# The last expert's last row of w_down multiplied by activations summed into tokens, and four stores of 256 KB

## What is computed

```python
def expert_block(args):
    e, toks, gw = args
    xb = h[toks]
    gu = xb @ w_gu[e] + b_gu[e]
    gate = jnp.minimum(gu[:, :D_FF], SWIGLU_LIMIT)
    up = jnp.clip(gu[:, D_FF:], -SWIGLU_LIMIT, SWIGLU_LIMIT)
    act = gate * jax.nn.sigmoid(gate * SWIGLU_ALPHA) * (up + 1.0)
    y = act @ w_down[e] + b_down[e]
    return (y * gw[:, None]).astype(h.dtype)
...
return jax.ops.segment_sum(y.reshape(n_slots, -1), slot_tok, num_segments=T)
```

## Time and profile before

| | |
|---|---|
| median of 3 runs | 989.25 us (989.24 to 989.61) |
| the profiled execution | 988.7 us |
| its span, first to last instruction | 986.9 us |
| mean granted TensorE clock | 0.987 |
| TensorE busy | 946.6 us, 96% |
| VectorE, ScalarE busy | 202.9 us, 127.7 us |
| HBM read | 416.80 MB, 423 GB/s over the span |

### The profile page before, as it was taken

How to read it: one execution, slowest core, us unless ns; L and a number is a source line. 1 busy time by engine, 2 the same in 40 slices (tenths; PEclk the granted TensorE clock), 3 DMA queues, 4 the chain that set the end, 5 groups by cost and what they waited for, 6 DMA issues and landing times.

```text
span 986.9 us, 11112 instructions
## 1 busy us (share of the span) xinstructions
PE 946.6 (96%) x4508; PEld 382.4 (39%) x4508; DVE 202.9 (21%) x610; ACT 127.7 (13%) x346; POOL 14.0 (1%) x9
## 2 busy tenths in 40 slices
PE   9999999999999899898989989889989999999997
PEld 5545433333333334333333333333333333333432
DVE  4645121212111121210112121011212112111121
ACT  2433111011110111010011101001101110011101
POOL 0031000000000000000000000000000000000000
PEclk9999999999999999999999999999999999999999
DMA  9999999999999999999999999999999999999996
GB/s 374 426 423 398 412 429 434 432 430 428 432 431 429 436 430 430 434 432 429 434 433 426 437 432 428 437 430 429 436 429 431 432 429 430 431 433 430 422 422 272
DMA packets 23869, 418.27 MB, mean 424 GB/s; under 512 B 2912, under 2 KB 3296, under 8 KB 8224
## 3 DMA queue, kind: packets, MB, share of 16 engines
q1 hardware_dynamic: 23408, 417.20, 99.2%
q10 hardware_dynamic: 432, 0.66, 0.2%
HBM read 416.80 MB, written 1.05 MB: 423 GB/s over the span
## 4 chain that ended last, share of the span: by engine, by line
PE 63%; DMA 36%; DVE 1%; issue 0%; ACT 0%; SPq 0%; DVEq 0%
DMA ring<-w_gu_dram 33%; PE ps L1237 29%; PE ps L1342 14%; PE ps L1205 4%; PE ps L1189 4%; DMA ring<-w_down_dram 3%; PE ps L1066 3%; PE ps L997 2%; PE ps L1004 1%; PE ps L1293 1%; PE ps L1301 1%; PE ps L1013 0%; PE ps L1039 0%; PE ps L1058 0%; PE ps L1046 0%
## 5 line engine op out<-in xcount | busy, mean ns | idle before, releaser
L1237 PE MATMUL ps<-ring,passing 128*64 128x512 f32 x1008 | 229.1, 604 | 14.8 <-DMA ring<-w_gu_dram 14.8
L1237 PE MATMUL ps<-ring,PR 128*64 128x512 f32 x976 | 224.5, 608 | 16.4 <-DMA ring<-w_gu_dram 16.2
L1342 PE MATMUL ps<-ring,PT 128*64 128x512 f32 x984 | 218.3, 595 | 0.5 <-DMA ring<-w_down_dram 0.5
L952 DVE TENSOR_SCALAR xw<-ps 128x256 f32<-128x256 f32 x64 | 27.2, 425 | 650.0 <-PE ps L1237 650.0
L1237 PEld LDWEIGHTS ps<-ring,passing 128*64 128x64 f32 x1008 | 76.8, 139 | 158.3 <-issue 143.8
L1237 PEld LDWEIGHTS ps<-ring,PR 128*64 128x64 f32 x976 | 74.9, 140 | 157.0 <-issue 145.4
L1342 PEld LDWEIGHTS ps<-ring,PT 128*64 128x64 f32 x984 | 68.1, 137 | 129.6 <-issue 127.5
L652 ACT ACTIVATE xw<-xw 128x256 f32<-128x256 f32 x64 | 26.6, 416 | 484.5 <-DVE xw L952 484.5
L1205 PE MATMUL ps<-PT 64*128 64x512 f32 x248 | 69.7, 640 | 0.0
L1189 PEld LDWEIGHTS ps<-qk,X 128*128 128x128 f32 x512 | 59.6, 191 | 18.8 <-issue 18.8
L1189 PE MATMUL ps<-qk,X 128*128 128x128 f32 x512 | 65.7, 281 | 0.0
(11 more groups left out here) (198 smaller groups left out, 374.6 us busy)
## 6 DMA issues: line engine op xcount, KB each, us to landing
ring<-w_gu_dram SPq DMA_DIRECT2D x48, 4096.0 KB, 28.2
ring<-w_down_dram SPq DMA_DIRECT2D x25, 4096.0 KB, 29.7
ring<-w_gu_dram SPq DMA_DIRECT2D x14, 2048.0 KB, 14.2
ring<-w_gu_dram SPq DMA_DIRECT2D x6, 3072.0 KB, 23.2
ring<-w_down_dram SPq DMA_DIRECT2D x5, 2048.0 KB, 23.1
ring<-w_gu_dram SPq DMA_DIRECT2D x9, 1024.0 KB, 9.6
ring<-w_down_dram SPq DMA_DIRECT2D x8, 1024.0 KB, 25.9
ring<-w_down_dram SPq DMA_DIRECT2D x2, 3584.0 KB, 27.6
```

Source lines behind the costliest of these rows:

```text
L952: nc.vector.tensor_scalar(gb[:, b, :], gu[:, b, 0, :], LIMIT, None, ALU.min).then_inc(g_ready, 1)
L1237: last = mm(ps[64 * j:64 * j + 64, GU + b, :], lhs, halves[j][:, 512 * b:512 * b + 512], start=start, stop=stop)
L1342: last = mm(ps[64 * j:64 * j + 64, bank, :], at[:, k, 64 * (c - GU_PIECES):64 * (c - GU_PIECES) + 64], rows[:, 512 * j:512 * j + 512], sta ...
```

## The change

Five things are changed, all of them behind the last gate and up.

1. Row 7 of expert 31 no longer goes through the slots' sum. TensorE first makes `a_tokens` (128 features x 256 tokens) from the activations in `gb` and the gates in `GT_last`, with one product of 64 slots x 128 features by 64 x 256. ScalarE copies it to SBUF. When row 7 has landed, four products of 128 x 128 by 128 x 512 add it to the four banks of the tokens directly.
2. The down sum of expert 31 ends with row 6 (`last_rows`), and ScalarE copies it then. Its four `to_tokens` calls are no longer two side by side but alternate with the four direct products, bank by bank. `acc_final` counts the second of each.
3. Expert 30's `to_tokens(0)` comes ahead of expert 31's rows 0 and 1, and `to_tokens(1)` ahead of rows 2 to 6.
4. `aT_last` moves from `gb`, which must now outlive it, to a free part of `extra`.
5. The output is stored in four transfers of 256 KB, the left halves by SP and the right halves by ScalarE's queue, each after its own copy. VectorE waits for its own bank alone (`2 * t + 1`).

```diff
--- before.py
+++ after.py
@@ -248,7 +248,8 @@
         of = PT[:, :, :].rearrange("p r s -> p (r s)")
         aT = cut(512, of).rearrange("p (f s) -> p f s", f=4)
         ye = cut(512, of)
-        aT_last, ye_last = gb.rearrange("p b (f s) -> p (b f) s", f=2), sg.rearrange("p b n -> p (b n)")
+        aT_last, ye_last = extra[:, 0, 0:512].rearrange("p (f s) -> p f s", f=4), sg.rearrange("p b n -> p (b n)")
+        a_tokens = extra[:, 1, 0:T * P]
         GT = cut(T * P, of).rearrange("p (t s) -> p t s", t=T)
         GT_last = cut(T * P, of).rearrange("p (t s) -> p t s", t=T)
         GdT = GT_last[0:2 * NE]
@@ -340,6 +341,7 @@
         aT_psum, aT_sb = sem("aT_psum"), sem("aT_sb")
         gt_psum, gt_sb, y_sb = sem("gt_psum"), sem("gt_sb"), sem("y_sb")
         more_done = sem("more_done")
+        a_tokens_psum, a_tokens_sb, last_rows = sem("a_tokens_psum"), sem("a_tokens_sb"), sem("last_rows")
         acc_final, out_a, out_v = sem("acc_final"), sem("out_a"), sem("out_v")
 
         block = ctx.enter_context(nc.Block())
@@ -503,12 +505,10 @@
 
             more_passes(sp, TURNS, next_pass)
 
-            sp.wait_ge(out_v, 1)
-            sp.wait_ge(out_a, 1)
-            sp.dma_start(out_t[0], X[:, 0, :]).then_inc(stored, 16)
-            sp.wait_ge(out_v, T)
-            sp.dma_start(out_t[1][:, 0:512], X[:, 1, 0:512]).then_inc(stored, 16)
-            sp.wait_ge(stored, 16 * 3)
+            for t in range(T):
+                sp.wait_ge(out_v, t + 1)
+                sp.dma_start(out_t[t][:, 0:512], X[:, t, 0:512]).then_inc(stored, 16)
+            sp.wait_ge(stored, 16 * 2 * T)
 
         @block.gpsimd
         def _(pool):
@@ -675,7 +675,10 @@
             nc.scalar.copy(aT_last, ps[:, GU, :].rearrange("p (f s) -> p f s", f=4)).then_inc(aT_sb, 1)
             gates_out(NE - 1, GT_last)
             down_out(NE - 2, GU_PIECES)
-            down_out(NE - 1, 0, GU + 1, ye_last)
+            act.wait_ge(a_tokens_psum, 1)
+            nc.scalar.copy(a_tokens, ps[:, GAT, T * P:2 * T * P]).then_inc(a_tokens_sb, 1)
+            act.wait_ge(last_rows, 1)
+            nc.scalar.copy(ye_last, ps[:, GU + 1, :]).then_inc(y_sb, 1)
 
             def next_pass(p, r):
                 for u in range(TURN):
@@ -692,8 +695,8 @@
             for t in range(T):
                 act.wait_ge(acc_final, 2 * t + 2)
                 nc.scalar.copy(X[:, t, 512:1024], ps[:, ACC[t] + 1, :]).then_inc(out_a, 1)
-            act.wait_ge(out_a, T)
-            act.dma_start(out_t[T - 1][:, 512:1024], X[:, T - 1, 512:1024]).then_inc(stored, 16)
+                act.wait_ge(out_a, t + 1)
+                act.dma_start(out_t[t][:, 512:1024], X[:, t, 512:1024]).then_inc(stored, 16)
 
 
         @block.vector
@@ -979,7 +982,7 @@
 
 
             for t in range(T):
-                dve.wait_ge(acc_final, 2 * t + 2)
+                dve.wait_ge(acc_final, 2 * t + 1)
                 nc.vector.tensor_copy(X[:, t, 0:512], ps[:, ACC[t], :]).then_inc(out_v, 1)
 
 
@@ -1341,14 +1344,20 @@
                         for j in range(2):
                             last = mm(ps[64 * j:64 * j + 64, bank, :], at[:, k, 64 * (c - GU_PIECES):64 * (c - GU_PIECES) + 64],
                                       rows[:, 512 * j:512 * j + 512],
-                                      start=c == GU_PIECES and k == 0, stop=c == PIECES - 1 and k == 3)
-                        if k == 3:
+                                      start=c == GU_PIECES and k == 0, stop=c == PIECES - 1 and k == (2 if step == "last" else 3))
+                        if step == "last" and c == PIECES - 1 and k == 2:
+                            last.then_inc(last_rows, 1)
+                        elif k == 3:
                             last.then_inc(pieces_used, 1)
                         elif step == "first" and c == GU_PIECES and k < 2:
                             last.then_inc(row_used, 1)
 
+                def last_row():
+                    pe.wait_ge(landed_end[u, GU_PIECES, KC - 1], 16)
+                    return piece(PIECES - 1, 4)[:, 3, :]
+
                 if last_two:
-                    return gate_up, between, turn_round, turn_gates, down
+                    return gate_up, between, turn_round, turn_gates, down, last_row
                 if step == "more":
                     if u % 2 == 0:
                         gather_own()
@@ -1384,26 +1393,32 @@
 
             for u in range(TURN - 2):
                 expert(TURNS - 1, u, early=TURN + u)
-            gate_up, between, _, _, down = expert(TURNS - 1, TURN - 2, "last but one")
+            gate_up, between, _, _, down, _ = expert(TURNS - 1, TURN - 2, "last but one")
             gate_up()
             between()
-            gate_up, _, turn_round, turn_gates, down_last = expert(TURNS - 1, TURN - 1, "last")
+            gate_up, _, turn_round, turn_gates, down_last, last_row = expert(TURNS - 1, TURN - 1, "last")
             gate_up()
             down(chunks=range(4))
             turn_round(GU)
             turn_gates()
             down(chunks=range(4, KC))
-            down_last(aT_last, GU + 1, range(2))
-            pe.wait_ge(gt_sb, NE - 1)
+            pe.wait_ge(gt_sb, NE)
+            mm(ps[:, GAT, T * P:2 * T * P], gb[64:128, 1, P:2 * P], GT_last[64:128].rearrange("p t s -> p (t s)"), start=True, stop=True, skip_group_check=True).then_inc(a_tokens_psum, 1)
             pe.wait_ge(y_sb, NE - 1)
             to_tokens(0)
-            down_last(aT_last, GU + 1, range(2, KC))
+            down_last(aT_last, GU + 1, range(2))
             to_tokens(1)
-            pe.wait_ge(gt_sb, NE)
-            pe.wait_ge(y_sb, NE)
+            down_last(aT_last, GU + 1, range(2, KC - 1))
+            pe.wait_ge(a_tokens_sb, 1)
+            row = last_row()
             for t in range(T):
-                for last in to_tokens(t, GT_last, ye_last):
-                    last.then_inc(acc_final, 1)
+                for j in range(2):
+                    direct = mm(ps[:, ACC[t] + j, :], a_tokens[:, t * P:(t + 1) * P], row[:, 512 * j:512 * j + 512], start=False, stop=True, skip_group_check=True)
+                    if t == T - 1 and j == 1:
+                        direct.then_inc(pieces_used, 1)
+                    if t == 0 and j == 0:
+                        pe.wait_ge(y_sb, NE)
+                    mm(ps[:, ACC[t] + j, :], GT_last[64 * j:64 * j + 64, t, :], ye_last[64 * j:64 * j + 64, :], start=False, stop=True, skip_group_check=True).then_inc(acc_final, 1)
 
             def next_pass(p, r):
                 for u in range(TURN):
```

## The result

| | before | changed |
|---|---|---|
| median | 989.24 us (7 runs, 988.4 to 990.02) | 992.37 us (7 runs, 992.12 to 993.88) |
| ratio of the comparison | | 1.0036, 95% interval 1.0026 to 1.0046 |
| profiled execution | 988.7 us | 992.48 us |
| its span | 986.9 us | 990.6 us |

By the ratio the changed kernel is slower by 3.6 us, between 2.6 and 4.6; the two medians lie 3.1 us apart.

What follows compares the result with a forecast made beforehand. Behind 970.8 the bound was taken to be TensorE's work: its end at 987.25 plus 3.64 us for the stores gives 990.9 against 986.9, +4.0 us; on the median 989.25 that is 993.2 us, range 991.6 to 994.4.

Steps and rivals of the forecast that it cites:

- TensorE's end, +5.2 us: TensorE's last product would end at 987.25 instead of 982.04, 5.2 us later.
- the eight products: Four direct products alternating with expert 31's four `to_tokens` calls at the end: 8 x 0.86 + 7 x 0.2 = 8.26 us.
- the start of `to_tokens(0)` behind the copy: Expert 30's `to_tokens(0)` would start 0.26 us behind ScalarE's copy of expert 30's sum, at 970.6.
- The 0.1 us that the prediction charged to that copy: In the kernel before, the copy of expert 31's sum, half covered by `to_tokens(1)`, was said to cost some 0.1 us.
- a call without partner: A `to_tokens` call between two full products on TensorE: 0.43 us from below, 0.86 from above; 0.86 was taken.
- The change of shape: Each switch on TensorE between full-height and half-height products among the last eight would cost 0.2 us, seven in all.
- The rival in which the changes cost nothing: Weights for the next of the last eight products load early, so seven shape changes are free: -1.4, 991.8; chance 0.12.
- the one in which an addition waits for the one before it in its bank: Each second product into a bank waits 0.16 us for the first, in four places: +0.7, 993.9; chance 0.10.
- The one in which the half-height products run in the shadow of the direct ones: Last eight products take 4.3 us instead of 8.26, as `to_tokens` streams beside full products: -4.0, 989.2; chance 0.07.
- The stores, -1.2 us: From TensorE's end to the span's end, 3.64 us instead of 4.86, as banks end about 2.1 us apart.
- a store that is alone: One 256 KB output store with no other beside it would take 2.4 us to land.
- The clock: Rival: TensorE's clock falls to half at 979, so the last eight products cost 7 us more: 1000; chance 0.04.

Runs made afterwards that it cites:

- The second group of runs: The changed kernel measured once more, unaltered, beside its variants on one chip: 992.30 us, ratio 1.0029 against the kernel before.
- staggered: Changed kernel with last products reordered: tile 0's direct ones and `to_tokens` pair, tile 1's pair, tile 1's direct ones; 990.86 us, ratio 1.0018 against the kernel before.
- the pairs: Changed kernel with the four direct products first, then the four `to_tokens` calls, j = 0 beside j = 1: 991.94 us, ratio 1.0027 against the kernel before.

## Why the prediction was right

**The bound.** TensorE, not the landing of row 7, was said to be the bound behind 970.8. It held for the changed kernel: the direct products began at 979.0, 0.6 us behind row 7's landing (978.46 in that execution). For the kernel before it was not quite so: its row 4 waited 0.17 us for the landing of rows 4 and 5 (first product at 975.77, where the distance of 0.43 us to the one before would have had it at 975.60), so that behind 975.8 it was TensorE. The forecast started from the measured end, 982.04, and took no harm.

**TensorE's end, +5.2 us.** Measured +5.3 in the profiled execution. The stream of loads was 0.24 us later in it than in the profiled one of before (row 7 of expert 30's end, 969.75 against 969.51), so the change itself made 5.1. Its parts: the eight products 8.34 us (forecast 8.26), the way up to them 0.2 us shorter than forecast. The term that was too large is the start of `to_tokens(0)` behind the copy: I gave it 0.26 us, as in the earlier trace rows, and it was 0.05 (copy until 970.55, product at 970.60). The 0.26 us were misread. In the kernel before `to_tokens(1)` held TensorE until 979.35 + 1.13 - 0.16 = 980.32, and that is when the first product of expert 31's `to_tokens` started: it did not wait for the copy at all. The 0.1 us that the prediction charged to that copy was not there either: the copy was hidden whole, and its cover in the changed kernel gained nothing.

**Prices.** The one that the earlier trace rows did not show, a call without partner, was chosen at its upper bound and measured at it: 0.86 us (two calls alone took the time of four). The change of shape, read from the earlier trace rows at 0.2 us, measured 0.2 us (seven of them 1.4 us, by leaving them out). The rival in which the changes cost nothing is excluded, and so is the one in which an addition waits for the one before it in its bank. The one in which the half-height products run in the shadow of the direct ones needed 4.3 us for the eight, and they took 8.3.

**The stores, -1.2 us.** Measured 3.24 us from TensorE's end to the span's end, against 3.64 forecast and 4.87 before: -1.6. The step that was off is the length of a store that is alone: 2.4 us was reckoned by taking 0.67 us of data off a store of 512 KB, and it was 2.0. The Trainium skill (DMA: Bandwidth & Descriptors, Anatomy of one DMA), by whose figures for another issuing path the estimate was 2.6 us, was further off. The forecast had 2.4 us for each of the four stores; they took 2.2, 4.0, 2.5 and 2.0 us. The second, at 4.0, lay outside what the prediction allowed the last one, and only its place in the order kept it out of the time. The mechanism was right: the splitting alone gave nothing (ratio 1.0000), 0.9 of the 1.6 us came with the old stores too, and the gain is bought with TensorE's slower end.

**Hidden things.** `a_tokens` and its copy, the copy of expert 31's sum and `aT_last` in `extra` cost nothing, as said: `a_tokens` stands in the wait for the copy of expert 30's sum, and behind 979.0 the products follow at one distance throughout.

**The clock** stayed at full until TensorE was done: in the changed kernel's stretch from 979 to 987 it was 1.00, and fell between 989 and 990.

```profile
979.00:987.00 8.00, 8.00 (x18) 2.37 (x16) 1.38 (x2) 1.17 (x2) 0.00 (x0) 1.00 0.19 68
...
989.00:990.00 1.00, 0.00 (x0) 0.00 (x0) 0.00 (x0) 0.00 (x0) 0.00 (x0) 0.63 0.70 262
```

Summed up: 5.3 - 1.6 = 3.7 us in the profiled execution, of which 0.24 is the stream's, so 3.4 to 3.5 for the change, in the middle of the measured 2.6 to 4.6. The second group of runs gave 3.0. The forecast of 4.0 was high by its store of 2.4 us above all.

## What to carry to other kernels

Before taking a copy or a sum out of a chain, count what the replacement costs on the engine that is already the bound. Here 0.86 us of half-width products side by side became 3.4 us of full-width ones, for a copy that another product already covered. Keep products of one shape together, and put a product that fills the whole array before or behind a group of half-array ones, not between them: here the order alone was worth 1.5 us of 992. A gain at the stores that comes from results being late is no gain, so read the drain from the end of the work and not by itself.

## What the runs showed that I had not expected

The two halves of the array took their calls independently over at least two calls: the order of the calls of different halves hardly mattered (1.99 us for eight instructions, against 1.88 where partners were neighbours).

The end of a store can hang on one DMA engine of sixteen (staggered: a share of 0.05 to 0.06 for its last 1.2 us). One packet of 16 KB on the instruction queue held an engine for 1.0 to 1.8 us in the last 7 us of these programs, and stores of 256 KB that were under way then took 3.2 to 4.0 us in the changed and the staggered kernel instead of 2.0 to 2.6. That the packet is the cause is an inference.

Four stores within 1 us took up to 4.65 us to land behind the pairs in the changed kernel, with 6.1 us from TensorE's end to the span's end, where three within 0.9 us took 3.5 and 4.9. In the kernel before, the same splitting gave 3.85 and 5.3 us and no difference in time (ratio 1.0000). So splitting the crowded stores gained nothing there. Whether it cost something behind the pairs is not shown, since no run has the old stores with that order.
